# Mixer bodies of a hybrid decoder layer: dense work in whole units between five groups of small matmuls

## What is computed

```python
x = x + 0.5 * post1(swiglu1(pre1(x)))                 # FFN, d_ff 2816
P = pre_m(x) @ w_in                                   # 2816 columns: attn q,k,v | hgrn q,f,i,g
A = sliding-window attention (window 128, sinks)      # 8 query heads, 2 kv heads, dim 64
f = lb + (1 - lb) * sigmoid(hf); logf = log(f)        # HGRN2 gates
# per chunk: G = cumsum(logf); o = (q*exp(G)) @ S + tril(q k decay) @ v
#            S = exp(G_end) * S + (k*exp(G_end - G)).T @ v
x = x + post_m(concat(A, H) @ w_out)
x = x + 0.5 * post2(swiglu2(pre2(x)))
```

## Time and profile before

| | us |
|---|---|
| median of 3 runs | 2115.23 (2111.83 to 2116.56) |
| the profiled execution | 2110.59, span 2108.8 |
| PE busy | 2046.0 (97%) |
| PEld busy | 1979.0 (94%) |
| DVE busy | 1097.2 (52%) |
| ACT busy | 581.0 (28%) |
| mean granted clock of PE | 0.995 |

### The profile page before, as it was taken

One profiled execution on the slowest core, in us unless ns is written; L12 is line 12 of the kernel. 1 busy time (PEld: TensorE's weight loads), 2 busy tenths in 40 slices (PEclk: granted clock), 3 DMA queues, 4 the chain that ended last, 5 costly groups with the idle time before them and its releaser, 6 DMA issues.

```text
span 2108.8 us, 33511 instructions
## 1 busy us (share of the span) xinstructions
PE 2046.0 (97%) x13575; PEld 1979.0 (94%) x13575; DVE 1097.2 (52%) x1927; ACT 581.0 (28%) x952; POOL 69.4 (3%) x34
## 2 busy tenths in 40 slices
PE   5999999999999998999999999999999999999996
PEld 5999999999999987998888899999999999999995
DVE  4543444444444467566666668644434444444446
ACT  5211111211111134145555655411111112111112
POOL 3000000000000003000000110100000000000000
PEclk9999999999999999999999999999999999999998
DMA  3211111111111113110010154111111111111111
GB/s 123 61 51 50 39 41 50 50 40 50 50 50 50 34 31 147 40 33 31 21 31 21 63 198 160 54 51 51 50 50 40 40 50 50 40 50 50 50 31 80
DMA packets 30127, 118.53 MB, mean 56 GB/s; under 512 B 3552, under 2 KB 4456, under 8 KB 28136
## 3 DMA queue, kind: packets, MB, share of 16 engines
q1 hardware_dynamic: 30056, 117.52, 17.2%
HBM read 106.67 MB, written 10.83 MB: 56 GB/s over the span
## 4 chain that ended last, share of the span: by engine, by line
PE 92%; DVE 4%; ACT 2%; issue 1%; DMA 0%; SPq 0%; DVEq 0%; ACTq 0%
PE PS L375 25%; PE PS L376 25%; PE PS L377 25%; PE PS L506 2%; PE PS L507 2%; PE PS L508 2%; PE PS L552 2%; PE PS L698 1%; DVE resid L1355 1%; PE PS L413 1%; PE PS L700 1%; PE PS L699 1%; DVE y L1350 1%; DVE x_lo L1363 1%; ACT sm L1119 1%
## 5 line engine op out<-in xcount | busy, mean ns | idle before, releaser
L375 PE MATMUL PS<-x_hi,w_hi 128*128 128x344 f32 x2280 | 733.0, 321 | 32.3 <-DVE w_lo L1337 22.0
L376 PE MATMUL PS<-x_lo,w_hi 128*128 128x344 f32 x2280 | 728.8, 320 | 0.0
L377 PE MATMUL PS<-x_hi,w_lo 128*128 128x344 f32 x2280 | 727.7, 319 | 0.0
L375 PEld LDWEIGHTS PS<-x_hi,w_hi 128*128 128x128 f32 x2280 | 429.5, 188 | 34.7 <-issue 21.9
L376 PEld LDWEIGHTS PS<-x_lo,w_hi 128*128 128x128 f32 x2280 | 429.6, 188 | 1.0
L377 PEld LDWEIGHTS PS<-x_hi,w_lo 128*128 128x128 f32 x2280 | 429.7, 188 | 0.0
L1454 DVE TENSOR_TENSOR y<-y,PS 128x344 f32<-128x344 f32 x528 | 264.4, 511 | 182.2 <-PE PS L377 182.2
L375 PE MATMUL PS<-h,w_hi 128*128 128x344 f32 x1056 | 339.7, 322 | 0.0
L376 PE MATMUL PS<-h,w_hi 128*128 128x344 f32 x1056 | 337.6, 320 | 0.0
L377 PE MATMUL PS<-h,w_lo 128*128 128x344 f32 x1056 | 336.7, 319 | 0.0
L895 ACT ACTIVATE w_hi<-raw 128x1024 fp32r<-128x1024 f32 x156 | 161.4, 1049 | 468.3 <-PE PS L377 464.2
(11 more groups left out here) (217 smaller groups left out, 1852.6 us busy)
## 6 DMA issues: line engine op xcount, KB each, us to landing
raw<-in_w_gu SPq DMA_DIRECT2D x88, 512.0 KB, 3.6
raw<-in_w_down SPq DMA_DIRECT2D x44, 512.0 KB, 3.6
raw<-in_w_in SPq DMA_DIRECT2D x22, 512.0 KB, 3.6
raw<-in_w_out SPq DMA_DIRECT2D x19, 512.0 KB, 3.7
resid<-in_x SPq DMA_DIRECT2D x3, 1376.0 KB, 9.3
stream_x<-resid SPq DMA_DIRECT2D x3, 1376.0 KB, 5.3
resid<-stream_x SPq DMA_DIRECT2D x3, 1376.0 KB, 7.8
out_y<-resid SPq DMA_DIRECT2D x3, 1376.0 KB, 4.7
```

Source lines behind the costliest of these rows:

```text
L375: nc.tensor.matmul(PS[:, bank, :GW], wh, vh, start=(k == 0), stop=False)
L376: nc.tensor.matmul(PS[:, bank, :GW], wh, vl, start=False, stop=False)
L377: mm = nc.tensor.matmul(PS[:, bank, :GW], wl, vh, start=False, stop=(k == last))
```

## The change

Three things are written in another order; no computation is added or removed.

PE: a unit is no longer cut. Five groups of small work a body stand between whole units of 24 matmuls, and `outputs` and `attend(1)` of a body are handed on (`end`) and issued at the head of the next body's first group.

```diff
-                def dense(s):
+                def dense(x):
                     units = body_units(i)
-                    if s // 2 < len(units) and units[s // 2] is not None:
-                        half_unit(units[s // 2], s % 2)
+                    if x < len(units):
+                        half_unit(units[x], 0)
+                        half_unit(units[x], 1)
...
-                dense(0)
+                ahead()
                 level(0)
-                dense(1)
+                masks(0)
+                scores(0)
+                level(1)
                 if b == 0:
                     values()
...
-                masks(0)
-                level(1)
-                scores(0)
-                dense(2)
+                dense(0)
                 level(2)
-                dense(3)
+                masks(1)
+                scores(1)
+                level(3)
...
-                level(3)
+                dense(1)
+                level(4)
+                keys_by_token()
+                dense(2)
+                states()
+                probs_by_key(0)
+                dense(3)
+                attend(0)
+                probs_by_key(1)
                 dense(4)
-                masks(1)
...
+                def end():
+                    outputs()
+                    attend(1)
```

```diff
                 decay(i, 3)
+                decay(i, 5)
...
+                exponentials(0)
                 decay(i, 4)
-                decay(i, 5)
...
                 divide(0)
+                exponentials(1)
                 unit_end(1)
...
                 nc.scalar.activation(kdT[:], PS[:, 7, :], ACT.Copy).then_inc(S["kdtc_done"], 1)
-                exponentials(1)
-                unit_end(2)
+                divide(1)
+                if b and t < TPH - 1:
+                    logs(t + 1)
```

```diff
+                decayed(i, 2)
+                if i:
                     weights_low(4, i - 1)
-                else:
+                weights(0)
+                sub_max(0)
+                weights(1)
+                if i == 0:
                     in_split(EARLY + 1)
                 level(i, 4)
-                decayed(i, 2)
                 decayed(i, 3)
-                weights(0)
-                weights(1)
+                over(0)
                 unit_end(0)
+                weights(2)
+                sub_max(1)
+                weights(3)
...
+                    elif g == 1 and n == 7:
+                        scan(0)
+                        level(0, 0)
+                        level(0, 1)
                     elif g == 0 and n == 8:
-                        scan(0)
-                        for l in range(4):
-                            level(0, l)
-            decayed(0, 0)
-            decayed(0, 1)
+                        level(0, 2)
+                        level(0, 3)
+                    elif g == 1 and n == 8:
+                        decayed(0, 0)
+                        decayed(0, 1)
```

More of the change, by code:

```diff
@@ L517, in head_sums, with body @@
                 mm.then_inc(S["css_done"], 1)
-            def body(i):
+            def body(i, ahead):
                 t, b, c = i // 2, i % 2, i
@@ L662, in body @@
                     head_sums(0, 2, TPH, 6)
-                level(3)
-                dense(4)
-                masks(1)
[L666 to L679, removed]
+                dense(1)
[7 more added lines that the diff above has]
+                probs_by_key(1)
+                dense(4)
+                def end():
+                    outputs()
+                    attend(1)
+                return end
             pe.wait_ge(S["mem_zero"], 1)
+            end = lambda: None
             for i in range(BODIES):
-                body(i)
+                end = body(i, end)
+            end()
             def out_part(k, a):
@@ L1067, in _ @@
             sigmoid(0)
+            logs(0)
             in_split(EARLY)
-            logs(0)
             first_decays(0)
@@ L1141, in body @@
                 decay(i, 3)
+                decay(i, 5)
+                act.wait_ge(S["scan_done"], TPH * (i + 1))
+                if i:
+                    act.wait_ge(S["o_done"], i)
+                nc.scalar.activation(dd[:, 7], gb, ACT.Exp).then_inc(S["dec7"], 1)
+                if i:
+                    act.wait_ge(S["st_done"], i)
+                nc.scalar.activation(g_end[:], gb[:, :, CH - 1], ACT.Exp).then_inc(S["gend_done"], 1)
+                exponentials(0)
                 decay(i, 4)
-                decay(i, 5)
                 if i == BODIES - 1:
@@ L1156, in body @@
                     sigmoid(t + 1)
[L1157 to L1164, removed]
                 unit_end(0)
-                if b and t < TPH - 1:
-                    logs(t + 1)
                 divide(0)
+                exponentials(1)
                 unit_end(1)
@@ L1185, in body @@
                     first_decays(i + 1)
-                divide(1)
-                if i < BODIES - 1:
                     decay(i + 1, 1)
                 unit_end(3)
+                if i < BODIES - 1:
+                    decay(i + 1, 2)
                 probs(1)
@@ L1192, in body @@
                     hi_hgrn(0)
-                if i < BODIES - 1:
-                    decay(i + 1, 2)
+                unit_end(4)
                 act.wait_ge(S["o_done"], i + 1)
@@ L1200, in body @@
                                      ACT.Copy).then_inc(S["attc_done"], 1)
-                unit_end(4)
             for i in range(BODIES):
@@ L1731, in body @@
                     scan(i + 1)
+                    level(i + 1, 0)
+                else:
+                    head_scaled(0)
                 unit_end(2)
-                if after:
-                    level(i + 1, 0)
-                    level(i + 1, 1)
-                over(1)
+                states()
                 weights_low(2)
                 if not after:
-                    head_scaled(0)
                     head_gated(0)
-                unit_end(3)
-                states()
-                if not after:
+                    unit_end(3)
                     weights_low(3)
                     return
-                if after:
-                    decayed(i + 1, 0)
-                    level(i + 1, 2)
-                    level(i + 1, 3)
-                    decayed(i + 1, 1)
+                level(i + 1, 1)
+                decayed(i + 1, 0)
+                level(i + 1, 2)
+                unit_end(3)
+                level(i + 1, 3)
+                decayed(i + 1, 1)
                 weights_low(3)
```

19 lines of the change are left out of this document (8 added, 11 removed).

## The result

| | before | after |
|---|---|---|
| median, us | 2113.53 (2110.64 to 2116.56, 4 runs) | 2100.01 (2099.68 to 2100.34, 4 runs) |
| profiled execution, span, us | 2108.8 | 2098.4 |
| mean granted clock of PE | 0.995 | 0.994 |

The changed kernel takes 0.9936 of the time, 95% interval 0.9919 to 0.9953: 13.5 us less. The forecast was 2101.3, 13.9 us less. Measured again beside later experiments (medians 2111.84 and 2100.23), the ratio was 0.9939 (0.9926 to 0.9952), 11.6 us. Two later executions, of 3381.8 and 2889.1 us at granted clocks of 0.56 and 0.66, are left out of every median here. The waits and the dense stretches did what was forecast; the small pieces, which the sum put at nothing, gave a part of it back.

A forecast was written before the change was run, and what follows sets the result against it. PE was taken as the bound, losing time to waits and dense/small borders. Borders -4.2, waits -11.1, body 0 +0.56 and +0.84 gave -13.9 us, from 2115.2 to 2101.3 us; range 2094 to 2109.

The forecast's parts named there:

- The bound and the sum: Eight bodies: PE bounds at clock 1.00; borders -4.2, waits -11.1, body 0 +0.56 and +0.84, sum -13.9 us.
- Waits removed, 11.1 us: PE's twelve waits, eight of them on exponentials(1), all go: 9.5 us listed, 11.1 with the overlap lost around them.
- Body 0, 0.84 and 0.56 us: New PE waits in body 0: 0.84 us before level(0) for bank 2's evacuation, 0.56 at level(1) behind half-wide masks and scores.
- No wait at `level(1)` and `level(3)`: Bodies 1 to 7: PE's work before level(1) and level(3) covers DVE's chains of 2.57 and 1.95 to 2.57 us.
- The borders, 4.2 us: Dense stretches fall from 78 to 39; each removed border saves a late first dense matmul, 0.107 us.
- Changes of shape: PE's small groups: each change costs some 0.1 us, 15 before, 16 after; rival that only they count: 2105.5 us, chance 0.18.
- The opening move: Body 0's first products moved to tiles 7 and 8, ahead of the last evacuation; up to 1.7 us more if DVE is late.
- The slower rival: ACT late to exponentials(0), PE stands at masks(1) and level(3); 2.2 us free, at 5 us late 2124 us; chance 0.05.
- a sign of being wrong: Stages outside the bodies: the forecast is wrong if they move by more than a microsecond.

The follow-up runs named there:

- ACT's order alone: Kernel before, with ACT's exponentials of the second half of the heads moved ahead of the kdT copy: bodies 281.0 us against 288.2, median 2103.5 us.
- masks first: Changed kernel with masks at the head of its first two groups, 13 changes of shape a body instead of 16: bodies 276.0 us against 276.2, median 2102.1 us.
- The border experiments: Changed kernel with half a dense unit moved between attend(1) and level(0), 2102.6 us, or between states and probs_by_key(0), 2101.0 us.
- ACT 8 us late: Changed kernel with 80 small extra activations on ACT ahead of exponentials(0) in each body: bodies 325.0 us against 276.2, one run of 2149.5 us.

## Why the prediction was right, point by point

- **The bound and the sum.** PE at full clock, waits and borders: confirmed, and the signs came: 39 dense stretches, `level(0)` to masks 1.09 us, the clock at 1.00. In the bodies -12.0 us stood against -13.9 in the sum, in the medians -13.5 and -11.6 us. That the forecast time of 2101.3 came within 1.3 us of the measured 2100.0 is in part luck. It started from 2115.2, the median of three executions; eleven later ones have 2111.8, seven of them between 2111.2 and 2112.7 and four between 2116.1 and 2116.4. From 2111.8 the same sum gives 2097.9, and the profiled execution, forecast at 2096.7, took 2100.2.
- **Waits removed, 11.1 us.** Right. All twelve are gone, and the run with ACT's order alone gives 7.2 us for the eight that were counted at 7.3. Counting by distances of starts, not by the listed idle time, was needed for that. What was missing: ACT's order and PE's distance both remove them, each alone.
- **Body 0, 0.84 and 0.56 us.** Right: 0.8 and 0.4 listed. By starts they are 925.19 - 924.07 - 0.16 = 0.96 and 0.5. PE started 0.25 us after the evacuation and not 0.12.
- **No wait at `level(1)` and `level(3)`.** No wait is listed in bodies 1 to 7, with 2.59 us against a chain of 2.57. But a chain that just fits isn't free: `level(1)` is released by DVE in every body and takes 1.02 us, where it takes 0.93 with the same neighbours and 0.42 us of room (masks first). That is about 0.7 us in all, which the sum put at nothing. For `level(3)` I gave 1.95 to 2.57; the run with `masks(1)` first puts it at about 2.0, against 2.54 available.
- **The borders, 4.2 us.** 12.0 - 11.1 + 1.5 = 2.4 us came back, 0.06 at each of 39 and not 0.107. To see where, I add up the distances between starts over the bodies of both traces, with the waits taken out:

| us | before | after |
|---|---|---|
| dense stretches | 158.7 | 154.4 |
| small pieces | 118.4 | 120.3 |
| waits, by starts | 11.1 | 1.5 |

The dense matmuls gave back 4.3 us, what the term said. The step that failed is the assumption that the small pieces stay as they are, because changes of shape, 15 and then 16, cancel: they take 1.9 us more. The changes do not cost the same everywhere. Before, all transposes but those of `values` stood alone among dense matmuls of their own shape, where the way in costs nothing. Now they stand behind pieces on half the array: in a steady body keys take 0.41 for 0.35, `states` 0.61 for 0.51, `probs_by_key` 0.85 for 0.79 twice, over the eight bodies 1.8 us more. The narrow `level`s take 0.8 more, most of it at the `level(1)` of the point above, and `attend` 0.4; scores and the head sums of body 7 give 1.1 back. The border experiments agree: 0.06 to 0.08 us where no shape changes, 0.2 to 0.25 at the border where two do.
- **Changes of shape.** The rows before were read as 0.09 us more for a `level` in front of another shape. That reading fails: `level(3)` now takes 0.94 us in front of a dense unit, behind scores, and the ones that stand behind dense matmuls take 1.04 whatever follows. The weighing of the Trainium skill's rule (TensorEngine Tiling (Array Packing), Key Properties: changing the mode drains TensorE) gave 2105.5 us had it been all. The trace agrees that a change costs, 0.08 us in the masks-first run; but borders without one cost 0.06 to 0.08 us too, so it is not all.
- **The opening move.** The forecast was right that it is needed and gave up to 1.7 us if DVE were late. It measured 3.9: the wait grew by less (1.0 us; the two wide products take 0.68 and 0.69 us on DVE, not 0.84 each), and the fall of the clock behind it was left out.
- **The slower rival.** Its place was right (`masks(1)`), its room of 2.2 us too small (some 5 us; with the 2 us of idle ACT that were counted before the last runs it is 4.2), and its price half of the true one, since it took a microsecond of waiting for a microsecond. With 3.0 us of wait a body the kernel lost 6.1, not 3.0.
- **Not foreseen.** The wait of 0.9 us at L516 in the output stage. It stood at 0.6 to 1.2 us in every profile of the changed order and its variants, and in neither trace of the old one. From the first dense matmul of the output projection to the end the kernel before took 897.5 us, the changed one 898.2 and, again, 898.7. The prediction had called it a sign of being wrong if the other stages moved by more than a microsecond; they stand at that limit, and it takes back a part of the 12.0 us of the bodies. ACT is late there because its split waits for the load of `o_raw`, 1.8 us now and 0.9 before, though the load is issued at the same point. Why it lands later was not tried.

## What to carry to other kernels

Read the distance between starts on a saturated TensorE, not only its idle time: a listed wait of 0.8 us cost 0.97, and the loss at a border or behind a chain that just fits appears in no list of waits. Group small matmuls so that neighbours use the same part of the array, and ask of each border whether it adds two changes of shape (0.2 to 0.3 us) or none (under 0.1). And look first for an in-order engine that stands at a wait with ready work behind it: here one such swap on ACT, alone, gave 7.2 us, where the whole change gave 12.

## What the runs showed of the hardware

- The granted clock can fall for a single short gap. 1.85 us of idle time in front of body 0 brought it from 2.4 to 1.2 GHz for some 7 us. It fell to 1.2 GHz too behind or within each of the eight waits of 1.88 to 3.56 us with ACT 8 us late, where each body became 1.5 to 4.4 us longer than by its wait. A wait of 1.83 us in body 1 of the kernel before left it at 1.00, and so did those of 0.8 us. What tells 1.83 from 1.85 us was not tried. PE was idle throughout both; dense matmuls stood in front of the one, dense matmuls and masks in front of the other.
- A narrow `level` behind scores that starts 0.14 to 0.17 us after DVE has released it takes 1.02 to 1.04 us to the next piece, with no idle time listed; one with 0.4 us of room or more takes 0.93 to 0.94. This holds for `level(1)` of the changed kernel against masks first, and for `level(3)` with a border in the first group (bodies 1, 3, 5 against 2, 4, 6, 7) and with `masks(1)` first. Why it costs 0.1 us inside the group of 16 was not taken apart.
